# One fp32 decoder block on one core: all projections with still activations, 512 weight columns per matmul and three products per column block

## The chip, the core and the metric

The kernel runs on one core of a Trainium2 chip. The metric is the device time of one execution in microseconds (us), as the median of repeated runs. TensorE (PE) does the matrix products and reads its operands from SBUF into PSUM; VectorE (DVE) and ScalarE (ACT) do elementwise work; GpSimd (POOL) only writes constants at the start; SyncE (SP) issues all DMAs.

## What is computed

`x` has 256 positions of 4096 channels, all in float32. The reference, cut to what matters:

```
u = rmsnorm(x, norm_w);  proj = u @ w_in            # w_in: 4096 x 24576
a_q, a_f, a_i, a_g, c_b, c_c, c_h, c_g (2048 each), g_a, g_b (4096 each) = split(proj)
f = lb + (1-lb)*sigmoid(a_f);  k = 1-f
y_a = rmsnorm(hgrn2(a_q, log f, k, a_i)) * silu(a_g)          # 16 heads of 128
y_b = c_b * causal_conv3(c_c * c_h) * silu(c_g)
merged = sigmoid(g_a + b0) * (y_a @ w_branch_a) + sigmoid(g_b + b1) * (y_b @ w_branch_b)
out = rmsnorm(x + merged @ w_out) * final_norm_w               # w_branch 2048 x 4096, w_out 4096 x 4096
```

The weights make 8192 tiles of 128 x 128 (6144 of `w_in`, 512 of each `w_branch`, 1024 of `w_out`), and each is multiplied with all 256 positions.

## The kernel before

**Three products for one.** Activations and weights are each kept as a high part, rounded to the type float32r, and a low part, the rest. A product is high x high + low x high + high x low. `U` holds for each of 32 channel tiles `[high 256 positions | low 256 positions]`; `Y` holds the two branch outputs in the same way.

**The weight stream.** SP loads chunks of 512 KB into four `RAW` buffers. ACT writes the high part into a ring of four buffers (`hi`, L321), DVE the low part (`lo`, L501), PE uses the chunk and counts `w_used`; ACT may write a ring buffer again when PE has used it. A chunk is 4 channel tiles (`KC = 4`) of 256 weight columns (`GW`), laid out `[256 high | 256 low]`. There are 1024 chunks. The ring buffers are `WH` in the HGRN stage, `WC` in the conv stage, `WM` in the merge stage, `WO` in the output stage; they are the same memory with a start moved by 192, 0, 128 and 64 bytes.

**How PE makes the three products.** In the mode `channels` the weights stand still: for each of two weight tiles one matmul with 512 moving columns (high weights past `[high | low]` of `U`, L869), then for each one with 256 (low weights past high `U`, L872). The result has channels on the partitions. In the mode `positions` the activations stand still: for each half of the positions 256 moving columns (low activations, high weights, L856) and 512 moving columns (high activations, `[high | low]` of the weights, L861). It is used for the values `V` of HGRN and for the output stage. In both modes a part of the sum lies in columns `T:2T` of the PSUM bank; ACT copies it out (`small_half`), and DVE adds both parts and multiplies by 1/rms (`drain_group`, L565 and L570). Every weight tile costs one matmul of 512 and one of 256 columns.

**Stages.** HGRN: 8 steps of 4 groups of 8 chunks (f, q, v, g for two heads); the attention of step a is spread over the chunks of step a+1: small matmuls on PE after chunks 4, 6, ... 18 and 22, a transpose of `O` after chunk 27 (L921), which waits for DVE's L664. Conv: 8 steps of 4 groups. Merge: 16 steps of 4 groups. Output: 16 groups. PE alternates between two PSUM pairs `PS[0]`, `PS[1]`. At the start `x` is transposed on PE (`turn_x`, L847), eight transposes between two chunks.

Of the kernel before, what the change touches and what calls it, by code (L numbers as in the profile page):

```python
# [18 lines left out]
KC = 4  # L41
# [3 lines left out]
NG = D // GW  # L45
XW = KC * P
XC = 1024
PERIOD = 256
AT_Y = 128
AT_HGRN, AT_CONV, AT_MERGE, AT_OUT = 192, 0, 128, 64  # L50
EARLY = 2
SLOTS = 16
# [3 lines left out]
A_Q, A_F, A_I, A_G, C_B, C_C, C_H, C_G = (BW * n for n in range(8))  # L56
G_A, G_B = 8 * BW, 8 * BW + D
HGRN_GROUPS = (A_F, A_Q, A_I, A_G)
CONV_GROUPS = (C_G, C_C, C_H, C_B)
X_AHEAD = ((4, 5), (6,), (7,), ())  # L60

TURNS_BRANCH = 4 * CD // RING
TURNS_MERGE = (2 * CD + 2 * CB) // RING
TURNS_OUT = 2 * CD // RING
CONV_TURN = NP * TURNS_BRANCH
MERGE_TURN = 2 * CONV_TURN
OUT_TURN = MERGE_TURN + NG * TURNS_MERGE
CONV_GROUP = 4 * NP
MERGE_GROUP = 2 * CONV_GROUP
OUT_GROUP = MERGE_GROUP + 4 * NG  # L70


def build(nc, x, norm_w, w_in, lb_logits, hgrn_norm_w, conv_w, w_branch_a, w_branch_b,
          gate_bias, w_out, final_norm_w, out):
    ctx = ExitStack()
    with ctx:
# [6 lines left out]
        def sem(name):  # L83
# [5 lines left out]
        region_y = region_u + KT * 2 * T * 4 + AT_Y  # L89
        region_m = region_y + 2 * KB * 2 * T * 4  # L90
# [6 lines left out]
        XR = at("XR", [P, 2, D], region_y + 2 * D * 4)  # L97
        MRG = at("MRG", [P, KT, T], region_m)
# [5 lines left out]
        ONES = at("ONES", [P, P], region_m + 8 * XW + 8 * P)  # L104
        VEC0 = at("VEC0", [KT, P], region_m + 8 * XW + 12 * P)
        W2 = 2 * T
        names = ["F", "V", "G", "SF", "SG", "PRE", "K", "SUF"]
        F, V, G, SF, SG, PRE, K, SUF = [at(n, [P, W2], region_m + 4 * W2 * i)
                                        for i, n in enumerate(names)]

        QX = at("QX", [P, 4, 192], region_m + 4 * W2 * len(names))
        QC = at("QC", [P, W2], region_m + 4 * W2 * len(names))
        scr = region_m + 4 * W2 * len(names) + 16 * 192
# [7 lines left out]
        RAW = [sb(f"RAW{i}", [P, KC, GW]) for i in range(RING)]  # L121
        ring = (nc.sbuf_base + PERIOD - 1) // PERIOD * PERIOD
        slot = KC * 2 * GW * 4 + PERIOD
        ctx.enter_context(nc.sbuf_tensor("ring", [P, (ring + RING * slot - nc.sbuf_base + 3) // 4], F32))

        def slots(stage, first):

            return [at(f"W{stage}{i}", [P, KC, 2 * GW], ring + i * slot + first, F32R) for i in range(RING)]

        W_HGRN, W_CONV = slots("H", AT_HGRN), slots("C", AT_CONV)  # L130
        W_MERGE, W_OUT = slots("M", AT_MERGE), slots("O", AT_OUT)
        SM = [sb(f"SM{i}", [P, 2, T]) for i in range(2)]
        GA, GB, Z = [sb(n, [P, W2]) for n in ("GA", "GB", "Z")]
        MASK = Z[:, 0:6 * 64]
        IDN = sb("IDN", [P, P])
        RB = sb("RB", [P, T])
        NW = GB[:, 64:64 + KT]
        VT1 = sb("VT1", [P, 96])
# [3 lines left out]
        LT = GB[:, 0:48]  # L142
        SSQ = sb("SSQ", [P, 2, NG])
# [5 lines left out]
        PS = [ctx.enter_context(nc.psum_tensor(f"PS{i}", [P, 2, 512], F32)) for i in range(2)]  # L149
# [8 lines left out]
        EPS_WRITTEN, IDN_WRITTEN, N_CONSTS = 1, 3, 19  # L158
# [6 lines left out]
        small_out = sem("small_out")  # L165
        drained = sem("drained")
        x_loaded = [sem(f"x_loaded{i}") for i in range(CD)]
# [8 lines left out]
        x_rstd = sem("x_rstd")  # L176
        x_spread = sem("x_spread")
# [6 lines left out]
        u_ready = sem("u_ready")  # L184
        gate_f = sem("gate_f")
        gate_g = sem("gate_g")
        level_ready = sem("level_ready")
# [6 lines left out]
        y_ready = sem("y_ready")  # L194
        merge_gate = sem("merge_gate")
        merged = sem("merged")
        m_hi = sem("m_hi")
        m_ready = sem("m_ready")
        xr_loaded = [sem(f"xr_loaded{i}") for i in range(2)]
        h_ready = sem("h_ready")  # L200
# [12 lines left out]

        block = ctx.enter_context(nc.Block())
# [3 lines left out]
        def _(sp):  # L218
# [6 lines left out]
            def load(w, rows, col, turn, s, free=True):  # L225
                src = w[rows * KC * P:(rows + 1) * KC * P, bass.ds(col, GW)]
                if free:
                    sp.wait_ge(lo_ready, RING * turn + s - (RING - 1))
                sp.dma_start(RAW[s][:, :, :], src.rearrange("(k p) c -> p k c", p=P)).then_inc(raw_loaded[s], 16)

            def column(i, col):


                return i * GW + col if col else (i + 1) * GW - GW

            def load_vectors():
                sp.dma_start(VEC1[0:32, :], lb_logits.rearrange("a (k p) -> (a k) p", p=P)).then_inc(vec_loaded, 16)
                sp.dma_start(VEC1[32:96, :], gate_bias.rearrange("a b (k p) -> (a b k) p", p=P)).then_inc(vec_loaded, 16)
# [3 lines left out]
            def branch(i, cols, turn0, first=False):  # L242
                for n, col in enumerate(cols):
                    col = column(i, col)
                    for c in range(CD):
                        if first and n == 0:
                            for j in ((c,) if c < RING else X_AHEAD[c - RING]):
                                load_x(j)
                            if c == CD - 1:
                                load_vectors()  # L250
                        load(w_in[0], c, col, turn0 + TURNS_BRANCH * i + (n * CD + c) // RING, c % RING,
                             free=not (first and n == 0 and c < RING))

            branch(0, HGRN_GROUPS, 0, first=True)
            with sp.Fori(1, NP) as i:
                branch(i, HGRN_GROUPS, 0)
            with sp.Fori(0, NP) as i:
                branch(i, CONV_GROUPS, CONV_TURN)
            with sp.Fori(0, NG) as i:
                turn = MERGE_TURN + TURNS_MERGE * i  # L260
                for n, col in enumerate((G_A, G_B)):
                    col = column(i, col)
                    for c in range(CD):
                        load(w_in[0], c, col, turn + (n * CD + c) // RING, c % RING)
                col = column(i, 0)
                for n, w in enumerate((w_branch_a, w_branch_b)):
                    for c in range(CB):
                        load(w[0], c, col, turn + (2 * CD + n * CB + c) // RING, c % RING)

            with sp.Fori(0, NG // 2) as i:  # L270
                for n in range(2):
                    col = column(i * 2 + n, 0)
                    for c in range(CD):
                        load(w_out[0], c, col, OUT_TURN + TURNS_OUT * i + (n * CD + c) // RING, c % RING)
                    if n == 0:
                        sp.wait_ge(w_used, RING * OUT_TURN)
                        sp.wait_ge(m_ready, CD)
                    cols = bass.ds(col, GW)
# [10 lines left out]
        def _(pool):  # L289
# [6 lines left out]
            pool.memset(ONES[:, :], 1.0).then_inc(consts, 1)  # L296
            pool.memset(AD[:, :, :], 0.0).then_inc(consts, 1)
            pool.memset(KL[:, :, :], 0.0).then_inc(consts, 1)
            pool.wait_ge(consts, 7)

            for n, m in enumerate(LEVELS[:6]):
# [3 lines left out]
                pool.wait_ge(consts, 8 + 2 * n)  # L305
# [6 lines left out]
        def _(act):  # L312
# [4 lines left out]
            def hi(ws, turn, s, free=True):  # L317
                act.wait_ge(raw_loaded[s], turn * 16 + 16)
                if free:
                    act.wait_ge(w_used, RING * turn + s - (RING - 1))  # L320
                act.activation(ws[s][:, :, 0:GW], RAW[s][:, :, :], ACT.Copy).then_inc(hi_ready, 1)  # L321

            def small_half(group, chunks, par, free=True, positions=False):
                act.wait_ge(w_used, chunks)
                if free:
                    act.wait_ge(drained, group - 1)
                if positions:
                    for b in range(2):
                        op = act.activation(SM[par][:, b, :], PS[par][:, b, T:2 * T], ACT.Copy, scale=ST[:, 12 + b:13 + b])
                    op.then_inc(small_out, 1)  # L330
                else:
                    act.activation(SM[par][:, :, :], PS[par][:, :, T:2 * T], ACT.Copy).then_inc(small_out, 1)

            act.wait_ge(gain_out, 1)
            for c in range(CD):

                for k in range(KC * c, KC * (c + 1)):
                    act.wait_ge(x_turned, k + 1)
                    act.activation(U[:, k, 0:T], XB[k % len(XB)], ACT.Copy, scale=NW[:, k:k + 1]).then_inc(u_hi, 1)
                hi(W_HGRN, c // RING, c % RING, free=c >= RING)  # L340

                act.wait_ge(x_loaded[c], 16)
                act.drain()
                act.activation(SQA[:, :], XS[:, 0, c * XW:(c + 1) * XW], ACT.Square,
                               accum_out=SSQ[:, 0, c:c + 1]).then_inc(x_sq, 1)
            def attention(a, slot):
                if slot == 1:

                    act.wait_ge(drained, 4 * a + 4)
                    act.activation(SG[:, :], G[:, :], ACT.Sigmoid).then_inc(gate_g, 1)  # L350
# [18 lines left out]
            def branch(i, turn0, group0, a=None, first=False, is_conv=False, after_it=None):  # L369
                own = W_CONV if is_conv else W_HGRN  # L370

                def ahead(c):

# [641 lines left out]
```

## Time and profile before

| | |
|---|---|
| median of 3 runs | 2955.69 us (2955.37 to 2956.11) |
| profiled execution, its own time | 2955.83 us |
| its span in the trace | 2954.1 us |
| PE busy | 2935.4 us (99%), 17061 matmuls |
| DVE, ACT busy | 1700.8 us (58%), 1308.3 us (44%) |
| mean granted clock of PE | 0.999 |
| DMA | 187 GB/s, 60% of the 16 engines' span |

The span goes from the first to the last instruction; the execution's own time is 1.7 us longer. The end of a matmul in the trace is modelled and overlaps the next one, so its duration (396 ns for 512 columns) is not what it costs; the distance from one start to the next is.

### The profile page before, as it was taken

What the parts mean: (1) busy time and instruction counts of PE and PEld (TensorE: products, weight loads), DVE (VectorE), ACT (ScalarE), POOL (GpSimd) and SP (SyncE); (2) the same over time, 40 slices, a digit from 0 to 9 for tenths busy, and PEclk for the clock granted to TensorE, in tenths of its full rate; (3) what the DMA queues carried; (4) which work ended last, traced back from release to release, by engine and by line L of the source; (5) the groups of instructions that cost most, each with busy time, mean ns of one, the idle gap of its engine ahead of it and who ended that gap; (6) DMA issues with size and microseconds to landing.
All of it is one profiled execution on the core that took longest, in us unless ns stands there. A gap on an engine that the chain in (4) does not pass through costs nothing.

```text
span 2954.1 us, 46544 instructions
## 1 busy us (share of the span) xinstructions
PE 2935.4 (99%) x17061; PEld 2572.9 (87%) x17061; DVE 1700.8 (58%) x1973; ACT 1308.3 (44%) x1523; POOL 6.9 (0%) x23
## 2 busy tenths in 40 slices
PE   9999999999999999999999999999999999999998
PEld 7888888888888888888888888888888888888887
DVE  7566665676665555555555555555555555655554
ACT  6444444444444444444444444444444444544444
POOL 0000000000000000000000000000000000000000
PEclk9999999999999999999999999999999999999999
DMA  7555555555556555566566666666666666666665
GB/s 242 180 177 166 171 176 177 165 172 174 173 171 191 187 190 186 179 196 192 186 191 186 190 186 190 185 191 186 190 186 190 186 190 186 189 203 208 202 204 190
DMA packets 550945, 552.32 MB, mean 187 GB/s; under 512 B 17217, under 2 KB 547826, under 8 KB 550898
## 3 DMA queue, kind: packets, MB, share of 16 engines
q1 hardware_dynamic: 550898, 551.71, 60.4%
q8 instruction: 27, 0.44, 0.1%
q14 instruction: 20, 0.16, 0.0%
HBM read 547.45 MB, written 4.19 MB: 187 GB/s over the span
## 4 chain that ended last, share of the span: by engine, by line
PE 99%; DMA 0%; DVE 0%; ACT 0%; issue 0%; ACTq 0%; SPq 0%; DVEq 0%
PE PS L869 52%; PE PS L872 26%; PE PS L861 12%; PE PS L856 6%; PE SC L906 1%; DMA XS<-in_x 0%; PE SS L906 0%; PE OB L915 0%; PE OB L916 0%; PE SC L896 0%; PE OB L914 0%; PE SS L921 0%; PE PS L847 0%; PE SC L847 0%; PE OB L847 0%
## 5 line engine op out<-in xcount | busy, mean ns | idle before, releaser
L501 DVE TENSOR_TENSOR WM<-RAW,WM 128x1024 fp32r<-128x1024 f32 x384 | 470.4, 1225 | 489.1 <-ACT WM L321 475.4
L321 ACT ACTIVATE WM<-RAW 128x1024 fp32r<-128x1024 f32 x384 | 407.5, 1061 | 605.1 <-PE PS L872 605.1
L869 PE MATMUL PS<-U,WC 128*128 128x512 f32 x2048 | 644.0, 396 | 0.0
L869 PE MATMUL PS<-U,WM 128*128 128x512 f32 x2048 | 638.0, 393 | 0.0
L869 PE MATMUL PS<-U,WH 128*128 128x512 f32 x1536 | 483.8, 396 | 0.5 <-DVE WH L501 0.5
L501 DVE TENSOR_TENSOR WC<-RAW,WC 128x1024 fp32r<-128x1024 f32 x256 | 312.2, 1225 | 282.9 <-ACT WC L321 273.7
L872 PEld LDWEIGHTS PS<-U,WC 128*128 128x128 f32 x2048 | 384.7, 188 | 90.9
L872 PEld LDWEIGHTS PS<-U,WM 128*128 128x128 f32 x2048 | 384.5, 188 | 89.2
L321 ACT ACTIVATE WC<-RAW 128x1024 fp32r<-128x1024 f32 x256 | 271.4, 1060 | 409.2 <-PE PS L872 409.2
L321 ACT ACTIVATE WH<-RAW 128x1024 fp32r<-128x1024 f32 x256 | 271.8, 1062 | 401.1 <-PE PS L872 273.4
L501 DVE TENSOR_TENSOR WH<-RAW,WH 128x1024 fp32r<-128x1024 f32 x256 | 311.6, 1224 | 227.8 <-ACT WH L321 217.4
L872 PE MATMUL PS<-U,WM 128*128 128x256 f32 x2048 | 406.1, 279 | 0.0
L872 PE MATMUL PS<-U,WC 128*128 128x256 f32 x2048 | 402.4, 278 | 0.0
L861 PE MATMUL PS<-WO,U 128*128 128x512 f32 x1024 | 359.1, 395 | 0.0
L872 PEld LDWEIGHTS PS<-U,WH 128*128 128x128 f32 x1536 | 289.0, 188 | 64.6
L869 PE MATMUL PS<-Y,WM 128*128 128x512 f32 x1024 | 321.4, 395 | 0.0
L869 PEld LDWEIGHTS PS<-U,WM 128*128 128x128 f32 x2048 | 312.8, 188 | 0.0
L869 PEld LDWEIGHTS PS<-U,WC 128*128 128x128 f32 x2048 | 311.8, 189 | 0.1
L872 PE MATMUL PS<-U,WH 128*128 128x256 f32 x1536 | 304.1, 279 | 0.0
L856 PE MATMUL PS<-WO,U 128*128 128x256 f32 x1024 | 285.5, 281 | 0.0
L501 DVE TENSOR_TENSOR WO<-RAW,WO 128x1024 fp32r<-128x1024 f32 x128 | 155.3, 1224 | 157.8 <-ACT WO L321 157.7
L869 PEld LDWEIGHTS PS<-U,WH 128*128 128x128 f32 x1536 | 234.5, 189 | 1.1 <-issue 0.7
(179 smaller groups left out, 2523.6 us busy)
## 6 DMA issues: line engine op xcount, KB each, us to landing
RAW<-in_w_in SPq DMA_DIRECT2D x768, 512.0 KB, 3.7
RAW<-in_w_out SPq DMA_DIRECT2D x128, 512.0 KB, 3.8
RAW<-in_w_branch_a SPq DMA_DIRECT2D x64, 512.0 KB, 3.7
RAW<-in_w_branch_b SPq DMA_DIRECT2D x64, 512.0 KB, 3.7
XS<-in_x SPq DMA_DIRECT2D x8, 512.0 KB, 9.7
XR<-in_x SPq DMA_DIRECT2D x16, 256.0 KB, 4.0
out_dram<-H SPq DMA_DIRECT2D x8, 512.0 KB, 4.0
FW<-in_final_norm_w SPq DMA_DIRECT2D x16, 128.0 KB, 3.8
```

Source lines behind the costliest of these rows:

```text
L321: act.activation(ws[s][:, :, 0:GW], RAW[s][:, :, :], ACT.Copy).then_inc(hi_ready, 1)
L501: dve.tensor_tensor(ws[s][:, :, GW:2 * GW], RAW[s][:, :, :], ws[s][:, :, 0:GW], ALU.subtract).then_inc(lo_ready, 1)
L856: return pe.matmul(bank[:, T:2 * T], stat_lo, both[:, 0:T], start=False, stop=stop, skip_group_check=True)
L861: op = pe.matmul(bank, stat_hi, both, start=first, stop=last, skip_group_check=True)
L869: pe.matmul(PS[par][:, t, :], w[:, k, t * P:(t + 1) * P], rhs[:, at_k, :], start=at_k == 0, stop=False, skip_group_check=True)
L872: op = pe.matmul(PS[par][:, t, T:2 * T], w[:, k, GW + t * P:GW + (t + 1) * P], rhs[:, at_k, 0:T], start=False, stop=at_k == n_tiles - 1, s ...
L906: op = pe.matmul(out, k_side, q_side, start=True, stop=True)
```

## The change

All projections now use still activations. A chunk is 2 channel tiles (`KC = 2`) of 512 weight columns (`OW`), again 512 KB, laid out `[512 high | 512 low]`, and there are still 1024 chunks. For each channel tile and each half of the positions, `product` issues three matmuls of 512 columns into the same PSUM bank: high activations x high weights, low activations x high weights, high activations x low weights. ACT's `small_half` and DVE's addition are gone, and 1/rms is a factor per partition. In HGRN and conv a group takes 256 columns of each of two projections (q and f; v and g; c_b and c_g; c_c and c_h), so that their chunks are loaded by two DMAs of 256 KB. What later code needs with channels on the partitions is transposed on PE: `turn_fq` (8 steps), `turn_conv` (8 steps) and `turn_merged` (8 steps), eight transposes each. Merge has 8 steps of 512 columns, output 8 groups. The gate bias is loaded per step and added by DVE. The four stage offsets of the ring are gone: every ring buffer, `U` and `Y` start at a multiple of 256 bytes. The core of the diff:

```diff
+OW = 512
-KC = 4
+KC = 2
-            def channels(par, w, rhs, k0, n_tiles):
-
-                for k in range(KC):
-                    at_k = k0 + k
-                    for t in range(2):
-                        pe.matmul(PS[par][:, t, :], w[:, k, t * P:(t + 1) * P], rhs[:, at_k, :],
-                                  start=at_k == 0, stop=False, skip_group_check=True)
-                    for t in range(2):
-                        op = pe.matmul(PS[par][:, t, T:2 * T], w[:, k, GW + t * P:GW + (t + 1) * P],
-                                       rhs[:, at_k, 0:T], start=False, stop=at_k == n_tiles - 1,
-                                       skip_group_check=True)
-                return op
+            def product(par, s, left, k0, n_tiles, halves=(0, 1)):
+
+                w = WS[s]
                 for k in range(KC):
                     at_k = k0 + k
+                    for b in halves:
+                        top, low = left[:, at_k, b * P:(b + 1) * P], left[:, at_k, T + b * P:T + (b + 1) * P]
+                        bank = PS[par][:, b, :]
+                        pe.matmul(bank, top, w[:, k, 0:OW], start=at_k == 0, stop=False)
+                        pe.matmul(bank, low, w[:, k, 0:OW], start=False, stop=False)
+                        op = pe.matmul(bank, top, w[:, k, OW:2 * OW], start=False, stop=at_k == n_tiles - 1)
                 return op
+            def turn_fq(i, first):
+
+                pe.wait_ge(drained, 2 * i + 1)
+                if first:
+                    pe.wait_ge(lb_ready, 1)
+                blocks = [GA[:, b, h * P:(h + 1) * P] for h in range(4) for b in range(2)]
+                for g in range(4):
+                    pe.transpose(SC[1][:, g * P:(g + 1) * P], blocks[g], IDN[:, :])
+                turn(SC[0], blocks[4:], fq_turned)
+                    if not is_conv and c == FQ_AT:
+                        turn_fq(i, first)
+                    if conv_of is not None and c == CONV_AT:
+                        turn_conv(conv_of)
...
+                    by_head = O[:, :].rearrange("p (h b e) -> p h b e", h=2, b=2)
+                    dve.tensor_tensor(by_head, by_head, SG[:, :].rearrange("p (b h e) -> p h b e", h=2, b=2),
+                                      ALU.mult).then_inc(o_ready, 1)
```

PE, the conv stage, before: the matmuls of one chunk, each row two matmuls of the mode `channels` (`WC_84` is a ring buffer).

```order
L872 MATMUL PS<-U,WC_84 128x256 x2
L869 MATMUL PS<-U,WC_84 128x512 x2
L872 MATMUL PS<-U,WC_84 128x256 x2
L869 MATMUL PS<-U,WC_84 128x512 x2
L872 MATMUL PS<-U,WC_84 128x256 x2
```

PE, the conv stage, now: the end of chunk 2 of a step, the eight transposes of `turn_conv` (four of `F`, four of `SG`), and the start of chunk 3 (`WS_56`, `WS_57` are ring buffers).

```order
L837 MATMUL PS<-WS_56,U 128x512
L838 MATMUL PS<-WS_56,U 128x512
L839 MATMUL PS<-WS_56,U 128x512
L899 MATMUL SC<-IDN,F 128x128 x4
L845 MATMUL SC<-IDN,SG 128x128 x4
L837 MATMUL PS<-WS_57,U 128x512
L838 MATMUL PS<-WS_57,U 128x512
L839 MATMUL PS<-WS_57,U 128x512
```

The matmuls of 256 columns are gone, every group of three has only 512, and a block of eight transposes stands between two chunks.

DVE in an HGRN step, around what PE waits for after chunk 27, before: the low part of a chunk, the last steps of the 1/rms of the head outputs, and the scaling of `O`.

```order
L501 TENSOR_TENSOR WH_80<-RAW,WH_80 128x4x256
L660 TENSOR_SCALAR RS<-RS 128x4
L485 RECIPROCAL RS<-RS 128x4
L487 TENSOR_TENSOR RS<-RS 128x4
L489 TENSOR_TENSOR RS<-RS 128x4
L491 TENSOR_SCALAR RS<-RS 128x4
L493 TENSOR_TENSOR RS<-RS 128x4
L664 TENSOR_TENSOR O<-OB,RS 128x512
```

The same place now:

```order
L483 TENSOR_TENSOR WS_55<-RAW_59,WS_55 128x2x512
L611 TENSOR_SCALAR RS<-RS 128x4
L466 RECIPROCAL RS<-RS 128x4
L468 TENSOR_TENSOR RS<-RS 128x4
L470 TENSOR_TENSOR RS<-RS 128x4
L472 TENSOR_SCALAR RS<-RS 128x4
L474 TENSOR_TENSOR RS<-RS 128x4
L615 TENSOR_TENSOR O<-OB,RS 128x512
L620 TENSOR_TENSOR O<-O,SG 128x512
```

The multiplication by the gate (L620) now stands ahead of the signal for PE.

## Rows read from the trace of the kernel before

**Rows 1.** The page: span, busy time of the engines, granted clock in 40 slices.

```profile
span 2954.1 us, 46544 instructions
PE 2935.4 (99%) x17061; PEld 2572.9 (87%) x17061; DVE 1700.8 (58%) x1973; ACT 1308.3 (44%) x1523; POOL 6.9 (0%) x23
PEclk9999999999999999999999999999999999999999
```

**Rows 2.** All waits of PE for other engines: total us, times, longest.

```profile
PE PS L838 <- DMA VEC<-in_norm_w: 2.7, 1, 2.7
PE PS L847 <- DMA XS<-in_x: 2.3, 1, 2.3
PE OB L847 <- DMA XS<-in_x: 1.5, 1, 1.5
PE PS L869 <- DVE WH L501: 0.5, 1, 0.5
```

**Rows 3.** The chain that ended last, share of the span by line.

```profile
by line: PE PS L869 52.2%; PE PS L872 26.2%; PE PS L861 12.1%; PE PS L856 6.2%; PE SC L906 1.4%; DMA XS<-in_x 0.2%; PE SS L906 0.2%; PE OB L915 0.1%; PE OB L916 0.1%; PE SC L896 0.1%; PE OB L914 0.1%; PE SS L921 0.1%; PE PS L847 0.1%; PE SC
```

**Rows 4.** Groups of instructions of the conv stage: count, busy us, mean ns, idle before.

```profile
L501 DVE TENSOR_TENSOR WC<-RAW,WC 128x1024 fp32r<-128x1024 f32 x256 | 312.2, 1225 | 282.9 <-ACT WC L321 273.7
L872 PEld LDWEIGHTS PS<-U,WC 128*128 128x128 f32 x2048 | 384.7, 188 | 90.9
L321 ACT ACTIVATE WC<-RAW 128x1024 fp32r<-128x1024 f32 x256 | 271.4, 1060 | 409.2 <-PE PS L872 409.2
```

**Rows 5.** Timeline of PE, conv stage: start, us, engine, line, what.

```profile
1000.34 0.62 PE L869 MATMUL PS<-U,WC 128*128 128x512 f32 x2
1000.80 0.40 PE L872 MATMUL PS<-U,WC 128*128 128x256 f32 x2
1001.03 0.63 PE L869 MATMUL PS<-U,WC 128*128 128x512 f32 x2
...
1005.21 0.63 PE L869 MATMUL PS<-U,WC 128*128 128x512 f32 x2
```

**Rows 6.** Timeline of PE, HGRN stage, mode channels.

```profile
299.82 0.62 PE L869 MATMUL PS<-U,WH 128*128 128x512 f32 x2
...
301.89 0.62 PE L869 MATMUL PS<-U,WH 128*128 128x512 f32 x2
```

**Rows 7.** Timeline of PE, mode positions: HGRN, then two places of the output stage.

```profile
180.84 0.28 PE L856 MATMUL PS<-WH,U 128*128 128x256 f32 x1
180.96 0.40 PE L861 MATMUL PS<-WH,U 128*128 128x512 f32 x1
181.19 0.28 PE L856 MATMUL PS<-WH,U 128*128 128x256 f32 x1
...
182.25 0.28 PE L856 MATMUL PS<-WH,U 128*128 128x256 f32 x1
...
2699.86 0.39 PE L861 MATMUL PS<-WO,U 128*128 128x512 f32 x1
...
2705.44 0.39 PE L861 MATMUL PS<-WO,U 128*128 128x512 f32 x1
...
2934.61 0.40 PE L861 MATMUL PS<-WO,U 128*128 128x512 f32 x1
...
2940.26 0.40 PE L861 MATMUL PS<-WO,U 128*128 128x512 f32 x1
```

**Rows 8.** Timeline of PE at the start: eight transposes between two chunks.

```profile
18.25 0.60 PE L847 MATMUL PS<-IDN,XS 128*128 128x128 f32 x4
18.68 0.60 PE L847 MATMUL SC<-IDN,XS 128*128 128x128 f32 x4
19.04 0.70 PE L869 MATMUL PS<-U,WH 128*128 128x512 f32 x2
19.58 0.40 PE L872 MATMUL PS<-U,WH 128*128 128x256 f32 x2
```

**Rows 9.** Timeline of DVE and PE at an HGRN step's transpose of O.

```profile
192.15 0.69 DVE L664 TENSOR_TENSOR O<-OB,RS 128x512 f32<-128x512 f32 x1
192.75 1.22 DVE L501 TENSOR_TENSOR WH<-RAW,WH 128x1024 fp32r<-128x1024 f32 x1
193.64 0.60 PE L921 MATMUL SS<-IDN,O 128*128 128x128 f32 x4
```

**Rows 10.** Timeline at the end: PE's last matmul, DVE's chain behind it.

```profile
2942.03 0.40 PE L861 MATMUL PS<-WO,U 128*128 128x512 f32 x1
2942.46 0.42 DVE L813 TENSOR_TENSOR SM<-PS,XR 128x256 f32<-128x256 f32 x1 [0.59 <-PE PS L861]
2946.39 1.42 DVE L831 TENSOR_SCALAR H<-H,ST 128x1024 f32<-128x1024 f32 x2
```

**Rows 11.** DMA issues of w_in: count, KB each, median us to landing.

```profile
RAW<-in_w_in SPq DMA_DIRECT2D x768, 512.0 KB, 3.7
```

More of the change, by code:

```diff
@@ L315, in _, with hi @@
             act.activation(ST[:, 19:20], EPT[:, :], ACT.Sqrt)
-            def hi(ws, turn, s, free=True):
-                act.wait_ge(raw_loaded[s], turn * 16 + 16)
+            def hi(chunk, s, free=True):
+                act.wait_ge(raw_loaded[s], (chunk - s) * (16 * KC // RING) + 16 * KC)
                 if free:
[L320 to L332, printed above, removed]
+                    act.wait_ge(w_used, chunk - (RING - 1))
+                act.activation(WS[s][:, :, 0:OW], RAW[s][:, :, :], ACT.Copy).then_inc(hi_ready, 1)
             act.wait_ge(gain_out, 1)
@@ new lines, in branch @@
+                    if is_conv and slot == 15:
+                        act.wait_ge(w_used, chunk0 + BRANCH * i + 2 * CD)
+                        act.wait_ge(drained, CONV_GROUP + 2 * i + 1)
+                        for b in range(2):
+                            op = act.activation(pair(SF)[:, b, :], PS[1][:, b, 0:T], ACT.Copy, scale=inv_rms(b))
+                        op.then_inc(gate_c, 1)
+            branch(0, 0, first=True)
+            with act.Fori(1, NP) as i:
+                branch(i, 0, a=i - 1)
@@ new lines, in _, with merge @@
+            branch(0, CONV_CHUNK, a=NP - 1, is_conv=True)
+            with act.Fori(1, NP) as i:
+                branch(i, CONV_CHUNK, is_conv=True)
+            def merge(i, first=False, last=False):
+                chunk = MERGE_CHUNK + MERGE * i
+                group = MERGE_GROUP + 4 * i
+                for c in range(MERGE):
+                    hi(chunk + c + RING, c % RING)
+                    if not first and c == MERGED_AT + 2:
+                        act.wait_ge(m_turned, i)
+                        for j in range(2):
+                            op = act.activation(MRG[:, bass.ds(i * 4 + 2 * j - 4, 2), :], pair(SC[j]), ACT.Copy)
+                        op.then_inc(m_kept, 1)
+                    if c in (CD + 1, 2 * CD + 1):
@@ L472, in _ @@
                         piece = H[:, b, c * XC:(c + 1) * XC]
[L473 removed]
+                        act.activation(piece, piece, ACT.Copy, scale=inv_rms(b)).then_inc(out_act, 1)
         @block.vector
         def _(dve):
[L478 removed]
             def after():
@@ L886, in attention, with turn @@
+                return op
+            def turn(bank, blocks, done):
+                for g, block in enumerate(blocks):
+                    op = pe.transpose(bank[:, g * P:(g + 1) * P], block, IDN[:, :])
+                op.then_inc(done, 1)
             def attention(a, c):
@@ L950, in branch @@
-            def branch(i, turn0, group0, modes, a=None, first=False):
-                for n in range(4):
-                    group(W_HGRN if turn0 == 0 else W_CONV, turn0 + TURNS_BRANCH * i, n * CD, CD, modes[n], U, 0, n % 2, group0 + 4 * i + n,
-                          free=not (first and n < 2), u_wait=(u_ready, KC) if first and n == 0 else None, a=a)
-            hgrn = (channels, channels, positions, channels)
-            branch(0, 0, 0, hgrn, first=True)
+                    pe.wait_ge(lo_ready, chunk0 + at_chunk + 1)
```

689 lines of the change are left out of this document (345 added, 344 removed).

## The prediction, made before the changed kernel was run

> **What bounds the kernel now.** I read the page first: PE is busy 99% of a span of 2954.1 us at full granted clock, DVE 58%, ACT 44% [rows 1]. Busy time says little where a matmul's end is only modelled, so I looked at PE's waits next: there are four, 7.0 us together, and all lie in the first 25 us [rows 2]. So no loaded chunk, no high or low part and no drain is late today. The chain that ended last says the same: 96.7% of it is the four lines of products, that is 2856.6 us [rows 3]. The kernel is a stream of matmuls on PE, and what counts is the distance from one start to the next. Each line's share gives it: the 512-column matmuls (L869, L861; 8192 of them, one for each weight tile) have 64.3% or 1899.5 us, so 231.9 ns each. The 256-column ones (L872, L856; 8192) have 32.4% or 957.1 us, so 116.8 ns each. At 2.4 GHz the columns alone are 213.3 and 106.7 ns. So 18.6 ns and 10.1 ns are paid above the columns.
>
> **The products.** A weight tile costs 768 columns now and will cost 768 columns: for two tiles, before 2 x 512 + 2 x 256, after 3 x 512. Three matmuls replace four, so 12288 matmuls of 512 columns replace 16384. The price of one is the question, and it decides everything: 1 ns on each is 12.3 us.
>
> From the shares: 3 x 231.9 = 695.7 ns against 2 x (231.9 + 116.8) = 697.4 ns. Over 4096 such triples that is 2849.6 us against 2856.6 us, so **-7.0 us**. Fewer matmuls bring little because what is paid above the columns grows nearly with the columns (18.6 to 10.1): only about 1.6 ns are left that are paid per matmul.
>
> The timeline lets me bound this price. Four `channels` matmuls (two of 512, two of 256) take 0.696 us in the conv stage (1000.34 to 1005.21, seven times) and 0.690 us in HGRN (299.82 to 301.89, three times) [rows 5, 6]. The mode `positions`, which the whole kernel now becomes, takes 0.705 us for the same columns in HGRN (180.84 to 182.25) and, in one and the same loop of the output stage, 0.698 us at one place (2699.86 to 2705.44, sixteen pairs of 0.349) and 0.706 us at another (2934.61 to 2940.26, sixteen of 0.353) [rows 7]. So the same code has two speeds 1.2% apart, and the moved starts of the ring go with others. The changed kernel has all starts at a multiple of 256 bytes, as only the conv stage has them now, and that one is in the middle. As a price of one 512-column matmul: the fastest of these (0.690) gives 230 ns by a third, the slowest (0.706) 235.3 ns. I take 231.9, the mean over the kernel, and keep 230 to 235.5 for the range: -30 to +37 us on the products.
>
> The weight loads: one stands ahead of every matmul, before and after, so 4096 fewer. A load's 188 ns [rows 4] lies under the running matmul. Under one of 256 columns (116.8 ns from start to start) that is tight, under one of 512 it is not. If it is the loads under the short matmuls that hold the stream back, their going is a gain that my mean over 512s does not hold; that is a rival below.
>
> The Trainium skill (TensorE: Matmul & The Clock Gate, Back-to-back issue gap) has a warm gap of N/2.4 + 2.5 ns, so 215.8 ns for 512 columns and 109.2 ns for 256. The trace disagrees by 16 and 8 ns for these fp32r operands. By the page's figures the products would go from 2662 to 2652 us, -10 us, nearly my step; the rule's fixed part is also all that it lets the change win.
>
> **The new transposes.** PE gets 24 blocks of eight (`turn_fq`, `turn_conv`, `turn_merged`, 8 each). Today's start shows such a block: it begins at 18.25, the next product at 19.04, and that one's pair has 0.54 us to its successor where 0.46 is usual, so 0.79 + 0.08 = 0.87 us [rows 5, 8]. 24 x 0.87 = **+20.9 us**. All of it is on PE's path and nothing covers it. Bounds: 0.79 (19.0 us) and 1.0 (24 us) if the way into and out of a block costs more. What goes: four small matmuls become two and the 1/rms spread vanishes at the start, -0.4 us. `turn_x` comes in fifteen blocks of four for seven of eight: eight more handovers of 0.08, +0.6 us.
>
> **Waits.** `turn_fq` stands 8 chunks behind its group (a chunk is four times 0.696 = 2.79 us), `turn_conv` and `turn_merged` 3 and 4. ACT and DVE need for the drain ahead of these: at most two ACT copies or a sigmoid, and two to four DVE instructions, each about 0.4 to 1.2 us by their elements, so 2 to 4 us against 8.4 and 11.2. They cost nothing. Behind DVE's longer waits (`w_used`, `gate_c`, `fq_turned`) stand its low parts. ACT makes a high part in 1.06 us and DVE a low part in 1.23 us [rows 4], both when PE has freed the buffer, three chunks (8.4 us) ahead of use. So 6 us of delay are covered, and per chunk ACT and DVE have 2.79 us for 1.06 and 1.23, so they catch up. The loads: 3.7 us for 512 KB [rows 11]; two of 256 KB double SP's issues to about 1 us per chunk, against 2.79. Nothing. If that cover were gone, 0.1 us per chunk would be 100 us, but I see nothing that eats 4 us of it steadily.
>
> The one tight wait is the transpose of `O` after chunk 27. DVE's L664 ends at 192.84, PE takes it at 193.64, 0.80 us of slack [rows 9]. The change puts a second 128x512 multiplication (0.69 us) and a drain of the pipeline in front of the signal, so some 0.05 us are left, while `turn_fq` after chunk 24 makes PE later too and ACT has one copy less in the way. I take 0; if none of the slack holds, 8 x 0.76 = 6 us.
>
> **The ends.** PE's first product may start 0.4 us earlier, with two channel tiles ahead of it in place of four. The tail, from PE's last start to DVE's last scaling, is 4.4 us [rows 10]. It loses one addition (0.42 us) and works on 512 columns for 256, three instructions of 0.69 for four of 0.42: +0.4 us. Together 0.
>
> **Sum.** -7.0 + 20.9 - 0.4 + 0.6 = **+14 us**. On the span, 2954.1 + 14.1 = 2968.2. The profiled execution took 1.7 us more than its span, and the median of the runs is 0.1 us below it. So 2955.7 + 14.1 = **2969.8 us**, 0.5% slower.
>
> **Rivals.**
>
> A, faster: the price above the columns is one of the handover from a matmul to the next, not of columns. On the four it is (18.6 + 10.1)/2 = 14.4 ns each, and the split 18.6 to 10.1 is only how a neighbour of the other length shifts the recorded starts. Then a 512 costs 227.7 ns, 12288 of them 2798 us, -59 +21 us, and the kernel takes 2918 us. For it: a load under every short matmul is tight. Against it: in `positions` every 256 stands alone between 512s and in `channels` they come in pairs, yet the totals for the same columns are 0.690 to 0.706 with the pairs no slower. It turns faster than before below a price of 230.7 ns. Chance 0.17.
>
> B, slower by more: the slow speed of `positions` (0.705) holds everywhere, because three matmuls in a row add into the same bank, or because still activations at these starts are the bad case. 235.5 ns each give 2894 us, +37 +21, so 3014 us. For it: both places with `positions` in HGRN and most of the output stage show it, no `channels` place does. Against: the same loop also runs at 0.698. Chance 0.2.
>
> C, my forecast (price 230.7 to 233.7, blocks 0.87): 0.53, and about 0.15 of it lies within 0.2% of before.
>
> D, the transpose of `O` or another new wait stalls PE: +6 us for the first; for a stall at every group more, up to +30. Chance 0.05, on top of any price.
>
> E, the short matmuls slow the whole stream, and a 512 between 512s comes down to its columns and the 1.6 ns per matmul: 215 ns, 2642 us, -215 +21, so 2762 us. The pairs of 512s in [rows 5] (0.46 us for two) speak against it. Chance 0.05. The gap of the Trainium skill (TensorE: Matmul & The Clock Gate, Back-to-back issue gap) would have it nearly so, at 215.8 ns; the trace's 231.9 does not.
>
> **Chances.** Faster by over 0.2%: A and E, and a little of C, 0.25. Within 0.2% (5.9 us; about what a measurement of this kernel can tell from no change): 0.15. Slower: 0.60. The range takes in A at its low end and most of B at its high: 2910 to 3010 us. The forecast's own range is 2955 to 2992.
>
> **What the profile of the changed kernel would show.** 12288 products with starts 231 to 233 ns apart, at the same distance in all stages, since all have the same starts of buffers; six of them per channel tile in 1.39 us. 24 blocks of eight transposes, 0.8 us each to the next product. PE's waits still in the first 25 us alone, DVE's L615/L620 just ahead of the transpose of `O`. DVE and ACT less busy, since `small_half` and one drain step are gone. Wrong would be: a distance that differs between stages or between the first, second and third product; a distance below 230; a wait of PE once per step.

## Result: 1.5% faster, where half a per cent slower was forecast

The changed kernel takes 2911.32 us (2910.32 to 2911.5) against 2955.9 us: a ratio of 0.9848, 95% interval 0.9831 to 0.9865. That is 44.6 us less; the forecast was 2969.8 us. The trace agrees with the runs: the span fell from 2954.1 to 2909.8 us.

The page after, lines that answer to [rows 1]:

```profile
span 2909.8 us, 39078 instructions
PE 2889.9 (99%) x13155; PEld 2399.8 (82%) x13155; DVE 1600.0 (55%) x1794; ACT 1232.0 (42%) x1326; POOL 6.7 (0%) x22
```

All waits of PE after, against [rows 2], and the chain by line, against [rows 3]:

```profile
PE PS L837 <- DVE WS L483: 3.6, 3, 2.7
PE PS L814 <- DMA VEC<-in_norm_w: 2.6, 1, 2.6
PE PS L823 <- DMA XS<-in_x: 2.2, 1, 2.2
```

```profile
by line: PE PS L837 32.1%; PE PS L839 31.9%; PE PS L838 31.9%; PE SC L868 1.4%; PE SC L845 0.4%; PE SS L868 0.2%; DMA RAW<-in_w_in 0.2%; DVE WS L483 0.1%; PE SS L845 0.1%; PE OB L877 0.1%; PE OB L878 0.1%; PE SC L858 0.1%; PE OB L876 0.1%; 
```

PE is still the bound, and its waits are 8.4 us in all, where they were 7.0. The three lines of products hold 95.9% of the span, 2790.5 us, where four lines held 2856.6 us: **-66.1 us**. All the rest of the chain grew from 97.5 to 119.3 us, **+21.8 us**. The shares are rounded to 0.1% of the span, so each of these sums is good to a few us; together they are the difference of the spans, -44.3 us, by construction.

Per matmul: the timeline of PE in the merge stage, first and last row of 26 that follow each other.

```profile
1699.81 0.39 PE L837 MATMUL PS<-WS,U 128*128 128x512 f32 x1
1700.04 0.39 PE L838 MATMUL PS<-WS,U 128*128 128x512 f32 x1
1700.27 0.39 PE L839 MATMUL PS<-WS,U 128*128 128x512 f32 x1
...
1705.48 0.39 PE L838 MATMUL PS<-WS,U 128*128 128x512 f32 x1
```

5.67 us over 25 distances are 226.8 ns. The columns alone take 213.3 ns at 2.4 GHz, so 13.4 ns are paid above them where I had 18.6. Times three that is 680 ns for the columns that cost 690 to 706 in [rows 5 to 7].

A new block of transposes (`turn_merged`) against the one in [rows 8]:

```profile
1639.75 0.60 PE L907 MATMUL SC<-IDN,GA 128*128 128x128 f32 x4
1640.18 0.60 PE L845 MATMUL SC<-IDN,GA 128*128 128x128 f32 x4
1640.54 0.48 PE L837 MATMUL PS<-WS,U 128*128 128x512 f32 x1
```

From the first transpose to the next product it takes 0.79 us, as forecast. The distances in the trace of the changed kernel give 0.79 us for each of the 24 new blocks, and the product behind a block has 0.315 us to its successor in place of 0.227. Together that is 24 x 0.88 = 21.1 us, so nearly all of the +21.8 us is the new transposes.

### The profile page after: what moved, and what is told of

It is laid out like the page before. It is cut to its first block, busy times and chain, and to the rows that moved or that the text cites. A ratio compares the mean times of both kernels' runs of the same rounds, so it can differ in the third digit from the quotient of the medians.

```text
span 2909.8 us, 39078 instructions
## 1 busy us (share of the span) xinstructions
PE 2889.9 (99%) x13155; PEld 2399.8 (82%) x13155; DVE 1600.0 (55%) x1794; ACT 1232.0 (42%) x1326; POOL 6.7 (0%) x22
## 4 chain that ended last, share of the span: by engine, by line
PE 99%; DVE 0%; DMA 0%; ACT 0%; ACTq 0%; DVEq 0%; issue 0%; SPq 0%
PE PS L837 32%; PE PS L839 32%; PE PS L838 32%; PE SC L868 1%; PE SC L845 0%; PE SS L868 0%; DMA RAW<-in_w_in 0%; DVE WS L483 0%; PE SS L845 0%; PE OB L877 0%; PE OB L878 0%; PE SC L858 0%; PE OB L876 0%; PE SC L899 0%; PE SC L891 0%; PE SC L907 0%
## 5 line engine op out<-in xcount | busy, mean ns | idle before, releaser
L483 DVE TENSOR_TENSOR WS<-RAW,WS 128x1024 fp32r<-128x1024 f32 x1024 | 1253.5, 1225 | 1249.1 <-ACT WS L314 1227.8
L314 ACT ACTIVATE WS<-RAW 128x1024 fp32r<-128x1024 f32 x1024 | 1084.6, 1060 | 1618.4 <-PE PS L839 1612.2
L837 PE MATMUL PS<-WS,U 128*128 128x512 f32 x3584 | 1408.2, 393 | 3.6 <-DVE WS L483 3.6
L839 PE MATMUL PS<-WS,U 128*128 128x512 f32 x3584 | 1397.7, 390 | 0.0
L838 PE MATMUL PS<-WS,U 128*128 128x512 f32 x3584 | 1397.0, 390 | 0.0
L837 PEld LDWEIGHTS PS<-WS,U 128*128 128x128 f32 x3584 | 673.8, 188 | 140.9 <-issue 3.7
L839 PEld LDWEIGHTS PS<-WS,U 128*128 128x128 f32 x3584 | 673.5, 188 | 140.9
L838 PEld LDWEIGHTS PS<-WS,U 128*128 128x128 f32 x3584 | 674.1, 188 | 136.0
L839 PE MATMUL PS<-WS,Y 128*128 128x512 f32 x512 | 199.3, 389 | 0.0
L838 PE MATMUL PS<-WS,Y 128*128 128x512 f32 x512 | 199.3, 389 | 0.0
L837 PE MATMUL PS<-WS,Y 128*128 128x512 f32 x512 | 199.3, 389 | 0.0
L839 PEld LDWEIGHTS PS<-WS,Y 128*128 128x128 f32 x512 | 96.1, 188 | 20.0
L837 PEld LDWEIGHTS PS<-WS,Y 128*128 128x128 f32 x512 | 96.1, 188 | 19.9
L838 PEld LDWEIGHTS PS<-WS,Y 128*128 128x128 f32 x512 | 96.1, 188 | 19.9
L868 PEld LDWEIGHTS SC<-QR,KL 128*126 128x126 f32 (+5 forms) x384 | 42.8, 173 | 6.5 <-issue 2.8
L868 PE MATMUL SC<-QR,KL 128*126 128x64 f32 (+5 forms) x384 | 42.5, 254 | 0.0
L565 DVE TENSOR_TENSOR PRE<-PRE 128x256 f32<-128x256 f32 x56 | 23.9, 426 | 4.6 <-issue 0.5
L553 DVE TENSOR_TENSOR KL<-K,SUF 128x256 f32<-128x256 f32 x56 | 23.3, 417 | 0.0
```

What stands on the lines that cost most here:

```text
L314: act.activation(WS[s][:, :, 0:OW], RAW[s][:, :, :], ACT.Copy).then_inc(hi_ready, 1)
L483: dve.tensor_tensor(WS[s][:, :, OW:2 * OW], RAW[s][:, :, :], WS[s][:, :, 0:OW], ALU.subtract).then_inc(lo_ready, 1)
L553: op = dve.tensor_tensor(halves(KL[:, n % 2, :], m)[0], halves(K[:, :], m)[0], s_left, ALU.mult)
L565: dve.tensor_tensor(p_right, p_right, over_left, ALU.mult)
L837: pe.matmul(bank, top, w[:, k, 0:OW], start=at_k == 0, stop=False)
L838: pe.matmul(bank, low, w[:, k, 0:OW], start=False, stop=False)
```

## The experiments

`e1_order` was run four times and `e7_before_start0` ten times; every other time below is of one execution. `e3_widths`, `e6_narrow` and `e10_uniform` leave out a part of the work, so only their distances count, not their totals (2647.9, 2861.9 and 2411.7 us).

Two theories stood against each other after the result. **Fixed price:** a matmul costs its columns and about 13.3 ns, so three in place of four save a fourth of that. **Surroundings:** what was new is which operands neighbours share, which bank they add to, or where the buffers start.

### Order and banks: no effect

`e1_order` is the changed kernel with the last two products exchanged:

```diff
-                        pe.matmul(bank, low, w[:, k, 0:OW], start=False, stop=False)
-                        op = pe.matmul(bank, top, w[:, k, OW:2 * OW], start=False, stop=at_k == n_tiles - 1)
+                        pe.matmul(bank, top, w[:, k, OW:2 * OW], start=False, stop=False)
+                        op = pe.matmul(bank, low, w[:, k, 0:OW], start=False, stop=at_k == n_tiles - 1)
```

> Only the order of the three products differs from the changed kernel: high x high, high activations x low weights, low activations x high weights, so that two matmuls in a row have the same still activations. Theory 1 (a matmul of 512 columns with its load fully under the one before costs its 213.3 ns and a fixed 13.3 ns, whatever stands around it): 226.7 ns per product as before, the time within 0.2% of 2911 us. Theory 2 (the price hangs on which operands neighbours share): a distance other than 226.7 ns in one of the three places, 1 ns of the mean being 12 us.

Measured: 2910.9 us, a ratio of 0.9849 (0.9832 to 0.9865) to before, so the same as the changed kernel. A second matmul with the same still activations is no cheaper; the trace has as many loads as matmuls, 13155 of each, as in the changed kernel.

`e2_banks` puts the loop over the halves inside the one over the three products:

```diff
-                    for b in halves:
...
+                    for which in range(3):
+                        for b in halves:
...
```

> The changed kernel, but the two halves of the positions alternate, so that no two matmuls in a row add into the same PSUM bank; the same moving columns are read twice in a row. Theory 1 (fixed price with the load covered): 226.7 ns still. Theory 2 (adding into the same bank in a row costs or saves something): the distance moves; at the 232 ns of the kernel before it would be 2976 us.

Measured: 2911.0 us, with 95.9% of a span of 2909.3 us in the products. Three additions in a row into one bank cost nothing. That takes one reason of my rival B away.

### Does the price grow with the columns?

`e3_widths` made the second and third product narrower, by stage:

```diff
+                        n = {'hgrn': 512, 'conv': 448, 'merge': 384, 'out': 320}[STAGE[0]]
...
-                        pe.matmul(bank, low, w[:, k, 0:OW], start=False, stop=False)
...
+                        pe.matmul(bank[:, 0:n], low, w[:, k, 0:n], start=False, stop=False, skip_group_check=True)
...
```

> Leaves out a part of the two small products: the second and third matmul of each three have 512 columns in the HGRN stage, 448 in conv, 384 in merge, 320 in output. The first stays at 512. Theory A (what is paid above the columns is fixed per matmul): distances of 226.7, 200.0, 173.3 and 146.7 ns, each 13.3 above its columns. Theory P (it grows with the columns, one part in 16): 226.7, 198.3, 170.0 and 141.7 ns. PE may wait for DMA in the last two stages, so the distances inside a chunk count, not the total.

Neither theory held. The merge stage, 512 and 384 columns:

```profile
1800.22 0.39 PE L840 MATMUL PS<-WS,U 128*128 128x512 f32 x1
1800.45 0.34 PE L842 MATMUL PS<-WS,U 128*128 128x384 f32 x1
1800.62 0.34 PE L843 MATMUL PS<-WS,U 128*128 128x384 f32 x1
...
1803.74 0.39 PE L840 MATMUL PS<-WS,U 128*128 128x512 f32 x1
```

Three matmuls take 3.52/6 = 587 ns, where the fixed price says 573 and the growing one 567. The 512s beside them now cost about 0.23 us. So a stream of several lengths costs more than its parts, and the distance after a 512 cannot be read as the price of a 512. That is just what I had done.

`e10_uniform` therefore gives all three products of a stage one width:

```diff
+                        n = {'hgrn': 512, 'conv': 384, 'merge': 320, 'out': 480}[STAGE[0]] if at_k else OW
+                        bank = PS[par][:, b, 0:n]
+                        pe.matmul(bank, top, w[:, k, 0:n], start=at_k == 0, stop=False, skip_group_check=True)
+                        pe.matmul(bank, low, w[:, k, 0:n], start=False, stop=False, skip_group_check=True)
...
```

> Leaves out columns: behind the first channel tile of a group all three products have 384 moving columns in conv, 320 in merge, 480 in output. HGRN stays at 512. The runs so far have 13.3 ns above the columns for streams of 512 alone and of 256 alone, but 16.0 for 448 alone. Theory A (fixed 13.3 ns if all matmuls have one length): 173.3, 146.7 and 213.3 ns. Rival (only lengths of 256 and 512 keep the two operand streams in step; any other length costs more): 176 ns or more, 149 or more, 216 or more.

First and last rows of three stretches without other work, of conv, merge and output:

```profile
949.82 0.33 PE L842 MATMUL PS<-WS,U 128*128 128x384 f32 x1
...
954.85 0.33 PE L841 MATMUL PS<-WS,U 128*128 128x384 f32 x1
...
1698.79 0.31 PE L840 MATMUL PS<-WS,Y 128*128 128x320 f32 x1
...
1703.19 0.31 PE L840 MATMUL PS<-WS,Y 128*128 128x320 f32 x1
...
2249.72 0.38 PE L842 MATMUL PS<-WS,U 128*128 128x480 f32 x1
...
2254.92 0.38 PE L842 MATMUL PS<-WS,U 128*128 128x480 f32 x1
```

29, 30 and 24 distances lie in them: 173.4, 146.7 and 216.7 ns. Above the columns (160.0, 133.3, 200.0) these are 13.4, 13.4 and 16.7 ns. The first two speak against a price that grows with the columns (it would be 170 and 142 ns); the last shows that a fixed 13.3 is the best case only and that some lengths cost some ns more.

### The same columns in more matmuls

`e4_split` splits matmuls of 512 in two of 256 with the same still operand:

```diff
+                        parts = {'hgrn': (512, 512, 256), 'conv': (512, 256, 256), 'merge': (256, 256, 256),
+                                 'out': (512, 256, 512)}[STAGE[0]]
+                        for still, c0, size in zip((top, low, top), (0, 0, OW), parts):
+                            for q in range(0, OW, size):
+                                op = pe.matmul(bank[:, q:q + size], still, w[:, k, c0 + q:c0 + q + size],
...
```

> The changed kernel with some matmuls of 512 columns split into two of 256 with the same still operand, so the columns stay and matmuls and loads are added: per three products 512,512,256,256 in HGRN, 512,256,256,256,256 in conv, six of 256 in merge, 512,256,256,512 in output. Theory A (fixed 13.3 ns per matmul): 256 columns cost 120.0 ns, the three products 693.3, 706.7, 720.0 and 693.3 ns. Theory P (one part in 16, load covered): 113.3 ns each, 680 ns in all four stages. Theory L (a load that lies under a short matmul holds the next one back): 512 keeps 226.7 unless a short one stands before it, and only stages with short ones go above 680, by an amount that grows with the number of loads under short matmuls.

One row of the merge stage (27 of 256 columns) and one of the output stage (70 matmuls of both lengths; such rows merge them under the form of the first):

```profile
1699.81 3.40 PE L844 MATMUL PS<-WS,U 128*128 128x256 f32 x27
...
2799.73 12.47 PE L844 MATMUL PS<-WS,U 128*128 128x512 f32 x70
```

With the last one's modelled 0.28 us off, (3.40 - 0.28)/26 = 120.0 ns for a 256 among 256s: 106.7 + 13.3, the same fixed price once more. In the output stage the row begins and ends with a 512, so its 69 distances are 17 fours (512, 512, 256, 256 in turn) and one more 512: (12.47 - 0.39 - 0.23)/17 = 0.697 us for four, where the fixed price has 0.693, and where three take 0.680 for the same columns. This stage is the old count and the old lengths with the new still activations and starts, and it is back at the old price ([rows 5] has 0.696). So the gain comes from the number of matmuls and their one length; the new still operand and the starts at 0 do not make it by themselves.

The whole kernel took 3052.24 us, 141 us more than the changed one; the fixed price alone makes 109 of it (13.3 ns for 1024 + 2 x 1024 + 3 x 1536 + 512 additional matmuls). Of the other 32 us, about 15 are waits of PE: six of 2.2 to 2.9 us stand ahead of the first product of a merge step. Behind each the granted clock is for a while at the lower of its two levels, 1.2 GHz of 2.4. The first of them, and the stretch behind it, whose mean granted clock is the 0.52, third number from the end:

```profile
1824.51 3.67 PE L844 MATMUL PS<-WS,U 128*128 128x256 f32 x16 [2.86 <-DVE WS L483]
```

```profile
1824.50:1828.00 3.50, 3.49 (x16) 3.50 (x17) 1.92 (x2) 0.00 (x0) 0.00 (x0) 0.52 0.56 156
```

Sixteen matmuls of 256 columns take about 3.5 us there, 213 ns from start to start in place of 120, and by their distances such matmuls cost some 10 us in all. What is left is of the size of what the mixed lengths cost. What causes the six waits is not known; the changed kernel has none there.

### Is it the load of the still operand?

`e6_narrow` has 448 columns in all products of conv, and still operands of 64 and 32 columns in merge and output:

```diff
+                        n, m = {'hgrn': (512, P), 'conv': (448, P), 'merge': (512, 64), 'out': (512, 32)}[STAGE[0]]
+                        if at_k == 0:
+                            n, m = OW, P
+                        bank = PS[par][0:m, b, 0:n]
+                        top, low = top[:, 0:m], low[:, 0:m]
...
```

> Leaves out work behind the first channel tile of each group: in the conv stage all three products have 448 moving columns (uniform), in merge the still operand has 64 columns in place of 128, in output 32; HGRN is unchanged. Theory A (13.3 ns fixed per matmul, and lengths that alternate cost extra, as the earlier run with 448 beside 512 had 205.0 and 230.0): 200.0 ns in conv. If the fixed part is the time in which a load of the still operand disturbs the stream, it falls with its columns in merge and output, to about 220 and 217 ns; if it is a handover from one matmul to the next, it stays 226.7 there.

Conv, merge, output:

```profile
1019.65 0.36 PE L844 MATMUL PS<-WS,U 128*128 128x448 f32 x1
...
1022.89 0.36 PE L845 MATMUL PS<-WS,U 128*128 128x448 f32 x1
...
1749.75 0.40 PE L844 MATMUL PS<-WS,U 128*64 128x512 f32 x1
...
1754.81 0.40 PE L845 MATMUL PS<-WS,U 128*64 128x512 f32 x1
...
2519.80 0.40 PE L846 MATMUL PS<-WS,U 128*32 128x512 f32 x1
...
2524.66 0.39 PE L846 MATMUL PS<-WS,U 128*32 128x512 f32 x1
```

Conv shows 16 distances of 202.5 ns, 15.8 above the columns (186.7), so 448 like 480 is a length that costs some ns more. Merge has 22 distances of 230.0 ns and output 21 of 231.4: more than with 128 still columns, not less. The loads did become shorter, from 188 to 134 and 109 ns (last number ahead of the second bar):

```profile
L845 PEld LDWEIGHTS PS<-WS,U 128*128 128x128 f32 x2096 | 394.4, 188 | 55.0
L845 PEld LDWEIGHTS PS<-WS,U 128*64 128x64 f32 x992 | 133.3, 134 | 93.2
L846 PEld LDWEIGHTS PS<-WS,U 128*32 128x32 f32 x496 | 54.0, 109 | 60.9
```

So a shorter load gives nothing back, and the 13.3 ns do not follow the load's length. But the shape of the load moved the price, by some 4 ns, so this is no clean separation. What the 13.3 ns are, a handover from one matmul to the next or something else, stays open.

### The starts of the buffers

`e5_start64`, `e5_start128` and `e5_start192` move only the ring of weight parts:

```diff
-        region_w = region_y + 2 * KB * 2 * T * 4
-        region_r = region_w + RING * KC * 2 * OW * 4
+        region_w = region_y + 2 * KB * 2 * T * 4 + 64
+        region_r = region_w + RING * KC * 2 * OW * 4 + 192
```

> The changed kernel with the whole ring of weight parts moved by 64 bytes; the kernel before had moved starts by stage and its stages differ (0.690 to 0.706 us for the same columns). Theory 1 (with only matmuls of 512 columns the price is 226.7 ns whatever the start): 2911 us within 0.2%. Theory 2 (the start sets part of the price in any stream): another distance; 1 ns is 12 us.

> The same with 128 bytes. Theory 1: 226.7 ns, 2911 us. Theory 2: another distance.

> The same with 192 bytes, the start of the HGRN stage before, which had the fastest channels matmuls. Theory 1: 226.7 ns, 2911 us. Theory 2: another distance; if the stage's 0.690 us for two short and two long ones came from its start, some 225 ns or less.

They took 2937.09, 2981.03 and 2988.29 us. The same stretch of the merge stage as above, for 64 and 192 bytes:

```profile
1699.65 0.39 PE L838 MATMUL PS<-WS,U 128*128 128x512 f32 x1
...
1704.92 0.39 PE L837 MATMUL PS<-WS,U 128*128 128x512 f32 x1
```

```profile
1699.73 0.39 PE L837 MATMUL PS<-WS,U 128*128 128x512 f32 x1
...
1704.87 0.39 PE L838 MATMUL PS<-WS,U 128*128 128x512 f32 x1
```

23 distances of 229.1 ns and 22 of 233.6 ns, against 226.8. So my first theory was wrong here: the start moves the price by between 6 and 7 ns per matmul at 192 bytes, 77 us in the sum, more than the whole gain. At 128 and 192 bytes the changed kernel is slower than before.

`e9_all64` moves `U`, `Y` and the ring together by 64 bytes:

```diff
-        region_u = base
+        region_u = base + 64
...
-        region_r = region_w + RING * KC * 2 * OW * 4
+        region_r = region_w + RING * KC * 2 * OW * 4 + 192
```

> The changed kernel with U, Y and the ring of weight parts all moved by 64 bytes, so that still and moving operands keep their distance. Moving the ring alone by 64 bytes gave 228.9 ns and 2937 us. If the distance between the two operands' starts sets the price: 226.7 ns, 2911 us. If each start for itself does: 228.9 ns or more, 2937 us or more.

2912.09 us; 23 distances in 5.22 us are 227.0 ns:

```profile
1699.72 0.39 PE L838 MATMUL PS<-WS,U 128*128 128x512 f32 x1
...
1704.94 0.39 PE L837 MATMUL PS<-WS,U 128*128 128x512 f32 x1
```

In this stream of 512s, and for this one shift, the distance between the starts of the two operands counts, not each start for itself.

Does the kernel before gain from starts at 0, too? `e7_before_start0`:

```diff
-AT_Y = 128
-AT_HGRN, AT_CONV, AT_MERGE, AT_OUT = 192, 0, 128, 64
+AT_Y = 0
+AT_HGRN, AT_CONV, AT_MERGE, AT_OUT = 0, 0, 0, 0
```

> The kernel before with all starts of ring buffers and of Y at a multiple of 256 bytes, as the changed kernel has them. Theory 1 (the gain comes from three matmuls for four and from equal lengths): conv unchanged at 697 ns for four, the other stages within 1.5% of what they had, the total 2950 to 2985 us, so not faster by more than 0.2%. Theory 2 (the gain comes from the starts at 0): most of the 44 us appears here, 2911 to 2925 us.

2955.63 us, a ratio of 0.9999 (0.999 to 1.0009). Nothing of the 44 us is in the starts alone: with all starts at 0, the kernel before takes 2955.6 us and the changed one 2911.3. The starts are a condition for the gain, as `e5` shows, not its source.

### Another order of the same matmuls

`e8_before_mix` alternates the lengths in `channels` and pairs them in `positions`:

```diff
-                    for t in range(2):
                         op = pe.matmul(PS[par][:, t, T:2 * T], w[:, k, GW + t * P:GW + (t + 1) * P],
...
+                    for low in ((False, True) if at_k == 0 else (True, False)):
+                        for b in halves:
...
```

> The kernel before with another order of the same matmuls: the mode channels alternates 512 and 256 columns in place of two and two, the mode positions takes two 256s, then two 512s, in place of alternating. Theory L (a change of length costs, so more changes cost more): channels rise from 690 to 697 ns for four towards 705, positions fall from 706 to about 697; three quarters and more of the products are channels, so the total rises to about 2985 us. Theory A alone (a fixed price per matmul): no stage moves, 2956 us within 0.2%.

2965.17 us, where theory L had 2985 and a fixed price alone 2956. The chain by line shows that both modes moved (L884 holds both lengths of `positions`):

```profile
by line: PE PS L869 52.2%; PE PS L871 26.6%; PE PS L884 18.0%; PE SC L909 1.4%; DMA XS<-in_x 0.2%; PE SS L909 0.2%; PE OB L918 0.1%; PE OB L919 0.1%; PE OB L917 0.1%; PE SC L899 0.1%; PE SS L924 0.1%; PE PS L847 0.1%; PE SC L847 0.1%; PE OB
```

Of a span of 2963.4 us, 78.8% for 6656 pairs of `channels` are 350.8 ns a pair, and 18.0% for 1536 of `positions` 347.3 ns. Before it was 78.4% and 18.3% of 2954.1 us [rows 3]: 348.0 and 351.9 ns. Pairing the lengths helps `positions`, alternating them costs `channels` on the whole. But not everywhere: in the conv stage, nine pairs now lie between

```profile
999.62 0.39 PE L869 MATMUL PS<-U,WC 128*128 128x512 f32 x1
...
1002.73 0.40 PE L869 MATMUL PS<-U,WC 128*128 128x512 f32 x1
```

so about 346 ns a pair, below the 348 of [rows 5]. Theory L in its simple form (every change of length costs) falls. The merge stage runs the same loop with its ring at 128 bytes, over `U`, which starts at 0, and over `Y`, which starts at 128:

```profile
1749.69 0.40 PE L869 MATMUL PS<-U,WM 128*128 128x512 f32 x1
...
1755.66 0.40 PE L869 MATMUL PS<-U,WM 128*128 128x512 f32 x1
```

```profile
1709.61 0.40 PE L869 MATMUL PS<-Y,WM 128*128 128x512 f32 x1
...
1715.97 0.40 PE L869 MATMUL PS<-Y,WM 128*128 128x512 f32 x1
```

17 pairs of 351 ns and 18 of 353 ns. So what a sequence of lengths costs goes with the starts as well. In conv and in the second of these, the ring and the other operand start alike (both at 0, both at 128), yet a pair costs 346 and 353 ns. So the rule that only the distance between the starts counts, which `e9_all64` gave for 512s, does not carry over to alternating lengths.

## Why the prediction was wrong

**The step that failed** is the price of a matmul: "From the shares: 3 x 231.9 = 695.7 ns". I took what the trace has between a 512's start and the next start as the price of 512 columns anywhere, and from 18.6 against 10.1 ns above the columns I read that the excess grows with the columns. Both numbers came from a stream in which 512s and 256s stand side by side, in pairs or in turn. In streams of one length they are 13.4 and 13.3 ns (`after`, `e4_split`). So the term "-7.0 us" should have been -66.1 us. 4096 matmuls fewer at 13.3 ns are -54.6 us of it. The other -11.5 us is what the old stream paid above the fixed price for its mixed lengths, 697.4 - 4 x 13.3 - 640 = 4.2 ns per four or 17 us, less some 5 us by which the new stream's share (681.3 ns for three) lies above its best 680. Why a stream of two lengths costs more than its parts is not known. The prediction's own sign of being wrong, "a distance below 230", is what the trace shows.

Rival A was the right mechanism, with 2918 us and a chance of 0.17: an equal price per matmul, and a split of 18.6 to 10.1 that neighbours of the other length make. Its 14.4 ns was the mean over the old mix, 1.1 ns too much. The argument that I held against it compared totals of 0.690 to 0.706 with each other; that they all hold four matmuls for the same columns, and so could not tell a price per matmul from one per column, I did not see. The measured 2911.3 us lies inside the range, at its very edge, only because the range was drawn wide enough to take in rival A; the forecast itself had the wrong sign.

**The transposes** were right: +20.9 us forecast, 21.1 us by the distances (+21.8 us for all that is not a product). **The waits** at the new transposes too: `turn_fq`, `turn_conv` and `turn_merged` cost none. The tight wait, DVE's L615 and L620 ahead of the transpose of `O`, in one step:

```profile
193.15 0.69 DVE L615 TENSOR_TENSOR O<-OB,RS 128x512 f32<-128x512 f32 x1
193.92 0.69 DVE L620 TENSOR_TENSOR O<-O,SG 128x512 f32<-128x512 f32 x1
194.67 0.42 PEld L845 LDWEIGHTS SS<-IDN,O 128*128 128x128 f32 x4 [0.22 <-DVE O L620]
194.71 0.61 PE L845 MATMUL SS<-IDN,O 128*128 128x128 f32 x4
```

L620 ends at 194.61, the load of the transpose comes at 194.67 after 0.22 us in which the load path stood idle, and PE itself shows no wait for it. The 0.80 us of slack in [rows 9] is used up, and nothing more: in no step is the distance from the last product to this transpose over 241 ns, 230 being usual. **The start** was right in part: the first product waits for the low part until 9.78 us, 0.6 us earlier than before (10.36) where 0.4 was forecast. But two more waits for a low part, at 60.6 and 64.2 us and so outside the first 25 us, together 0.9 us, take that back.

```profile
9.78 0.77 PE L837 MATMUL PS<-WS,U 128*128 128x512 f32 x1 [2.72 <-DVE WS L483]
```

**Rival B** (the slow price of 235 ns) did not come, but `e5_start192` comes near it with about 233.5 ns in a kernel that differs only in the start of the ring. Its argument that most of the output stage runs at the slow speed was a misreading: of 511 groups of four matmuls there, 225 take 0.709 to 0.711 us and about half 0.696 to 0.700. The forecast that all stages would show one distance, since all have the same starts, was right (the output stage has 23 distances in 5.21 us, 226.5 ns, beside the merge stage's 226.8):

```profile
2699.64 0.39 PE L837 MATMUL PS<-WS,U 128*128 128x512 f32 x1
...
2704.85 0.39 PE L839 MATMUL PS<-WS,U 128*128 128x512 f32 x1
```

But I had the reason only half: with another distance between `U` and the ring it would have been one slow distance. The Trainium skill (TensorE: Matmul & The Clock Gate, Back-to-back issue gap) gives the gap of an isolated matmul at the full clock as N/2.4 + 2.5 ns, which for 512 columns makes an estimate of 215.8 ns. The traces do not agree: no stream of 512s here, of these fp32r operands, comes nearer than 226.7.

## What to carry to other kernels

In a saturated TensorE stream count matmuls, not only columns: here each cost 13.3 ns above its columns in a uniform stream of 256, 320, 384 or 512, with both operands starting at a multiple of 256 bytes. So of these lengths the longest moving operand wins, even at the price of transposes (21 us spent, 66 saved). Never take a price per length from a stream of mixed lengths; fit it to the total, or run a stream of one length. And when an operand's layout changes, try the start of one buffer against the other in steps of 64 bytes, since that alone was worth 77 us here and can turn the verdict.

## What the hardware showed that was not expected

- Three uniform lengths cost their columns and 13.3 ns to within 0.1 ns (320, 384, 256), and 512 226.8 ns, but 448 and 480 cost 15.8 and 16.7 ns above.
- Moving one operand's buffer by 64, 128 or 192 bytes against the other's cost 26, 70 and 77 us; moving both by 64 cost 0.8 us (0.03%, one execution).
- A still operand of 64 or 32 columns in place of 128 made the loads shorter (134 and 109 ns for 188) and the matmuls 3 to 5 ns slower.
- Alternating 512s and 256s took 346, 351 and 353 ns a pair in one and the same loop, with the starts of ring and moving operand at 0 and 0, 128 and 0, 128 and 128 bytes.
- The order of the three products and the PSUM bank that they add into made no difference that can be measured (2910.9 and 2911.0 against 2911.3 us).
